# FFN up projection on Trainium2: one 512-column moving operand for both halves of x, and a sum of two bank halves on ScalarE and VectorE

## The chip, the core and the metric

The kernel runs on one core of one Trainium2 chip. The metric is the device time of one execution in microseconds. Before the change three executions gave a median of 713.83 us (712.39 to 713.88).

## What is computed

A decoder trunk of two layers over x of 256 tokens by 1024 columns, in float32. Each layer has a mixer (a short gated convolution beside an attention group) and a feed-forward part. The change touches the feed-forward part alone:

```
u = _causal_dwconv(x @ w_up[i], ffn_conv_w[i]) + ffn_conv_b[i]        # width 3, along the tokens
val, gate = u[..., :D_FF], u[..., D_FF:]                               # D_FF = 2816
x = _layer_norm(ALPHA * x + (jax.nn.silu(gate) * val) @ w_down[i], ln2_g[i], ln2_b[i])
```

## The kernel before

**Products.** A float32 product is made of three matmuls in the type f32r: each operand is split into a high part (a copy rounded to f32r) and a low part (the rest), and the product is high by high, high by low and low by high. The helper `mm3` (lines 1154, 1155 and 1156) issues the three, so these three lines carry nearly all matmuls of the kernel. The weights are split by ScalarE (`split_hi`, line 286) and VectorE (`split_lo`, line 290), unit by unit: a unit is 128 by 2048 elements. Raw units arrive by DMA from SP's queue in three buffers, and split units lie in six slots. x is split into `xh` and `xl`, each of 8 blocks (k) of 256 tokens.

**Feed-forward steps.** The 2816 inner columns are worked in 11 steps (s = 0 to 10) of 256. A step has two up units, value (v = 0) and gate (v = 1), and one down unit. For steps 1 to 10 the weights are the stationary operand and x is the moving one, so that the products come out with the inner columns on the partitions: `up` makes, for each v, two groups (c = 0 and 1, 128 inner columns each) of 8 k by 3 matmuls with 256 moving columns. Both groups of a v lie side by side in one bank, and the steps take turns: bank 4+2·odd+v. So a step may start its matmuls as soon as VectorE has finished with the step before last (`fy_done` of G-2, G counts the steps over both layers). Step 0 is done by rows (`up_rows`, x stationary), copied out by ScalarE (`copy_rows`, line 518) and transposed back (`rows_transposed`, line 1395) into banks 4 and 5.

**ScalarE and VectorE in a step.** ScalarE makes the convolution's first term with the bias from the bank (line 532, two instructions for each v), VectorE adds the other two taps from the bank (line 962, eight instructions: tap 1 of v = 0, tap 1 of v = 1, tap 2 of v = 0, tap 2 of v = 1, two groups each). Then ScalarE takes silu of the gate (line 541), VectorE multiplies (line 971), ScalarE and VectorE split the result h into `hTh` (line 548) and `hTl` (line 977); in the last step these are `qTh` and `qTl`. Between these, each of the two engines has up to three units of weights to split (`units`), at fixed places of its program: after the taps, after the product, after the split of h. GpSimd copies the step's parameters (line 693).

**Order.** Each engine's program is a fixed list. TensorE's is: rows of step 0, transposes, up 1, up 2, down 0, up 3, down 1, up 4, and so on, to up 10 and `down_last`, in which the down products of steps 8, 9 and 10 are interleaved so that the products with h of step 10 come late. VectorE's and ScalarE's program goes step by step, and each must finish step s (with its splits) before it begins step s+1:

```
up(L, 1, 1, (21, 0), (22, 0))
up(L, 2, 0, (23, 0), (24, 0))
down(L, 0, 0, (25, 0))
up(L, 3, 1, (26, 0), (27, 0))
```

Of the kernel before, what the change touches and what calls it, by code (L numbers as in the profile page):

```python
# [24 lines left out]
P = 128  # L25
D_MODEL, SEQ, DEPTH, HEAD = 1024, 256, 2, 64
KT = D_MODEL // P
# [9 lines left out]
STEPS = D_FF // (2 * P)  # L37
# [84 lines left out]
FY_CREDIT = 4  # L122

H_CREDIT = 2


def build(nc, x, w_in, short_conv_w, cmp_pe, cmp_w1, cmp_b1, cmp_w2, cmp_b2, head_norm_g, w_out, ln1_g, ln1_b,
          w_up, ffn_conv_w, ffn_conv_b, w_down, ln2_g, ln2_b, consts, out):
    fp32, f32r, bf16 = mybir.dt.float32, mybir.dt.float32r, mybir.dt.bfloat16
    ALU, ACT, AX = mybir.AluOpType, mybir.ActivationFunctionType, mybir.AxisListType  # L130

    with ExitStack() as ctx:
        def sb(name, shape, dt=fp32):
            return ctx.enter_context(nc.sbuf_tensor(name, shape, dt))

        def sem(name):
            return ctx.enter_context(nc.semaphore(name))
# [4 lines left out]
        ring_lo = [sb(f"ring_lo{i}", [P, UNIT], f32r) for i in range(SLOTS)]  # L142
        x_tok = sb("x_tok", [P, TT, D_MODEL])

        xh = sb("xh", [P, KT, SEQ], f32r)
        xl = sb("xl", [P, KT, SEQ], f32r)
        hTh = sb("hTh", [P, 2, 2, SEQ], f32r)
        hTl = sb("hTl", [P, 2, 2, SEQ], f32r)
        qTh = sb("qTh", [P, NPAIR, SEQ], f32r)
# [25 lines left out]
        part = work[:, 1024:2048].rearrange("p (t f) -> p t f", t=TT)  # L175
        ffn_y = work[:].rearrange("p (s v c n) -> p s v c n", s=2, v=2, c=2)
# [30 lines left out]
        conv_y = sb("conv_y", [P, 2, SEQ])  # L207
        conv_o = sb("conv_o", [P, 4, SEQ])

        conv_sq = sb("conv_sq", [P, 2, SEQ])  # L210
        rope_a, rope_b = (conv_sq[:, n, 0:14 * ROPE].rearrange("p (h d) -> p h d", h=14) for n in range(2))
        cstat = sb("cstat", [P, 2, TT, 4])
# [10 lines left out]
        rstd = sb("rstd", [P, TT])  # L223
        CMP_BANK = (7, 2)

        XT_BANK, MIX_BANK, X1T_BANK, ROWS_BANK, FFN_BANK = (4, 6), (4, 0), (4, 2), (6, 0), (0, 2)
        bank = [ctx.enter_context(nc.psum_tensor(f"bank{i}", [P, 512], fp32)) for i in range(8)]


# [29 lines left out]
        ln_stats, ln_root = sem("ln_stats"), sem("ln_root")  # L259
        step_par_in, fy_init = sem("step_par_in"), sem("fy_init")  # L260
        fy_mid, fy_done = sem("fy_mid"), sem("fy_done")
        rows_done, rows_copied, rows_T = sem("rows_done"), sem("rows_copied"), sem("rows_T")
        silu_done, h_done, h_hi, h_lo = sem("silu_done"), sem("h_done"), sem("h_hi"), sem("h_lo")
        y2_done = sem("y2_done")
        passed = sem("passed")
        dve_seq, pool_seq = sem("dve_seq"), sem("pool_seq")


        def xT_turn(L, t, b):

# [8 lines left out]
        def unit_used(eng, L, u, i=0):  # L279

            eng.wait_ge(slot_free[slot_of(L, u)], CREDIT + slot_round(L, u, i) + 1)
# [112 lines left out]
        def _(act):  # L394
# [125 lines left out]
            def ffn_step(L, s, odd, value, gate, h_user, units, dst=None):  # L520


                G = L * STEPS + s
                act.wait_ge(step_par_in, G + 1)
                act.wait_ge(h_lo, H_CREDIT + G - 1)
                for v, u in enumerate((value, gate)):
                    if isinstance(s, int) and s == 0:
                        act.wait_ge(rows_T, 2 * L + v + 1)
                    else:
                        unit_used(act, L, *u)  # L530
                    for c in range(2):
                        ins = nc.scalar.activation(ffn_y[:, odd, v, c, :], bank[4 + 2 * odd + v][:, SEQ * c:SEQ * (c + 1)],  # L532
                                                   ACT.Identity, scale=step_par[:, odd, v, c, 2:3],
                                                   bias=step_par[:, odd, v, c, 3:4])
                    ins.then_inc(fy_init, 1)
                for u in units[0:1]:
                    if u:
                        split_hi(act, *u)
                act.wait_ge(fy_done, FY_CREDIT + 2 * G + 2)
                y = ffn_y[:, odd].rearrange("p v c n -> p v (c n)")  # L540
                nc.scalar.activation(y[:, 1], y[:, 1], ACT.Silu).then_inc(silu_done, 1)
                for u in units[1:2]:
                    if u:
                        split_hi(act, *u)
                act.wait_ge(h_done, G + 1)
                if h_user:
                    unit_used(act, L, *h_user)
                nc.scalar.activation((hTh[:, odd] if dst is None else dst).rearrange("p c n -> p (c n)"), y[:, 0],
                                     ACT.Copy).then_inc(h_hi, 1)
                for u in units[2:3]:  # L550
                    if u:
                        split_hi(act, *u)
# [171 lines left out]
        def _(dve):  # L724
            V = nc.vector
            dve.sem_inc(fy_done, FY_CREDIT)
            dve.sem_inc(h_lo, H_CREDIT)
            V.memset(warm[:], 1.0).then_inc(warm_ready, 1)
            dve.sem_inc(x_ready, 4)

# [220 lines left out]
            def ffn_step(L, s, odd, value, gate, units, hi=None, lo=None):  # L951

                G = L * STEPS + s
                for back in (1, 2):
                    for v in range(2):
                        b = bank[4 + 2 * odd + v]
                        if back == 1:
                            dve.wait_ge(fy_init, 2 * G + v + 1)
                        else:
                            dve.wait_ge(fy_mid, 2 * G + v + 1)  # L960
                        for c in range(2):
                            ins = V.scalar_tensor_tensor(ffn_y[:, odd, v, c, back:], b[:, SEQ * c:SEQ * (c + 1) - back],  # L962
                                                         step_par[:, odd, v, c, 2 - back:3 - back],
                                                         ffn_y[:, odd, v, c, back:], ALU.mult, ALU.add)
                        ins.then_inc(fy_mid if back == 1 else fy_done, 1)
                for u in units[0:1]:
                    if u:
                        split_lo(V, *u)
                dve.wait_ge(silu_done, G + 1)
                y = ffn_y[:, odd].rearrange("p v c n -> p v (c n)")  # L970
                V.tensor_tensor(y[:, 0], y[:, 0], y[:, 1], ALU.mult).then_inc(h_done, 1)
                for u in units[1:2]:
                    if u:
                        split_lo(V, *u)
                dve.wait_ge(h_hi, G + 1)
                hi, lo = (hTh[:, odd], hTl[:, odd]) if hi is None else (hi, lo)
                V.tensor_tensor(lo.rearrange("p c n -> p (c n)"), y[:, 0], hi.rearrange("p c n -> p (c n)").bitcast(fp32),
                                ALU.subtract).then_inc(h_lo, 1)
                for u in units[2:3]:
                    if u:  # L980
                        split_lo(V, *u)
# [169 lines left out]
        def _(pe):  # L1151
            def mm3(dst, ah, al, bh, bl, start, stop, **kw):

                pe.matmul(dst, ah, bh, start=start, stop=False, **kw)  # L1154
                pe.matmul(dst, ah, bl, start=False, stop=False, **kw)  # L1155
                return pe.matmul(dst, al, bh, start=False, stop=stop, **kw)  # L1156
# [232 lines left out]
            def rows_transposed(L):  # L1389

                for t in range(TT):
                    for v in range(2):
                        pe.wait_ge(rows_copied, 4 * L + 2 * t + v + 1)
                        for c in range(2):
                            ins = pe.transpose(bank[4 + v][:, SEQ * c + P * t:SEQ * c + P * (t + 1)],
                                               probs[t][:, SEQ * v + P * c:SEQ * v + P * (c + 1)], ident)
                        if t:
                            ins.then_inc(rows_T, 1)

            def up(L, s, odd, value, gate):  # L1400

                G = L * STEPS + s
                for v, u in enumerate((value, gate)):
                    wait_unit(L, *u)
                    pe.wait_ge(fy_done, FY_CREDIT + 2 * (G - 2) + v + 1)
                    wh, wl = w_view(L, u[0], KT)
                    for part in range(2):
                        for c in range(2):
                            for k in range(4 * part, 4 * part + 4):
                                ins = mm3(bank[4 + 2 * odd + v][:, SEQ * c:SEQ * (c + 1)], wh[:, k, P * c:P * (c + 1)],  # L1410
                                          wl[:, k, P * c:P * (c + 1)], xh[:, k, :], xl[:, k, :], k == 0 and c == 0, k == KT - 1,
                                          skip_group_check=True)
                    free_unit(ins, L, u[0])

            def down_product(L, s, odd, u, t, n, c):
# [53 lines left out]
            for L in range(DEPTH):  # L1469
# [6 lines left out]
                for t, first, b in in_order:  # L1476
                    tok = slice(P * t, P * (t + 1))
                    u = first + b
# [179 lines left out]
```

## Time and profile before

| | |
|---|---|
| median of three executions | 713.83 us |
| the profiled execution's own time | 709.42 us |
| its span, first to last instruction | 707.6 us |
| mean granted TensorE clock | 0.985 |
| TensorE matmul busy | 690.6 us, 98% |
| TensorE weight load busy | 631.8 us, 89% |
| VectorE busy | 492.1 us, 70% |
| ScalarE busy | 345.1 us, 49% |
| GpSimd busy | 158.6 us, 22% |
| HBM read | 115.19 MB, 164 GB/s over the span |

Matmuls are pipelined and their ends are modelled: the duration of one overlaps the next. The time that a matmul costs is therefore read from start to start, and a full busy share only says that matmuls follow one another. ScalarE and VectorE instructions of one group overlap a little too (by some 0.1 us).

### The profile page before, as it was taken

The page shows a single profiled execution, that of the slowest core. Times are in us where ns is not written, and L with a number is a line of the kernel's source. Part 1 is how long each engine was busy: PE and PEld are TensorE (multiplying, and loading weights), DVE is VectorE, ACT ScalarE, POOL GpSimd, SP SyncE. Part 2 cuts the span into 40 slices and gives each one's busy share as a digit, 9 for nine tenths or more (in the row PEclk, how much of TensorE's full clock was granted, in tenths as well). Part 3 has the DMA queues.
Part 4 walks back from the last instruction along what each step waited for, and adds up shares of the span by engine and source line. Part 5 has one row for each costly group of instructions (what it writes and reads, how often), then busy time and mean ns, then how long its engine had stood idle before and what let it go on. Part 6 is the DMA issues. An engine that isn't in the chain of part 4 may idle for free.

```text
span 707.6 us, 11957 instructions
## 1 busy us (share of the span) xinstructions
PE 690.6 (98%) x4822; PEld 631.8 (89%) x4822; DVE 492.1 (70%) x698; ACT 345.1 (49%) x492; POOL 158.6 (22%) x54
## 2 busy tenths in 40 slices
PE   8999999999999999999999999999999999999995
PEld 5899999888999999999778999988889999999994
DVE  4675768877996666666786457686869766666646
ACT  5654535414865444444347444453258555555520
POOL 0000020230174444440000000113106444444300
PEclk9999999899999999999999999997999999999998
DMA  9972443333875555556248143432357755555301
GB/s 290 323 249 62 142 156 119 120 119 106 282 241 195 191 195 196 194 188 179 78 148 269 61 150 118 152 102 78 119 200 245 269 179 179 179 178 178 119 0 60
DMA packets 87403, 116.85 MB, mean 165 GB/s; under 512 B 5230, under 2 KB 73536, under 8 KB 87360
## 3 DMA queue, kind: packets, MB, share of 16 engines
q1 hardware_dynamic: 85920, 111.85, 47.3%
q10 hardware_dynamic: 1440, 4.39, 1.8%
q8 instruction: 30, 0.49, 0.3%
q14 instruction: 13, 0.11, 0.0%
HBM read 115.19 MB, written 1.05 MB: 164 GB/s over the span
## 4 chain that ended last, share of the span: by engine, by line
PE 92%; DVE 5%; DMA 1%; issue 1%; ACT 1%; SPq 0%; DVEq 0%; ACTq 0%
PE bank L1154 28%; PE bank L1155 27%; PE bank L1156 27%; PE bank L1239 3%; PE bank L1226 2%; DMA x_tok<-in_x 1%; PE bank L1175 1%; DVE x_tok L941 1%; DVE stats L925 1%; DVE x_tok L923 1%; PE bank L1218 1%; DVE ring_lo L290 1%; DVE x_tok L949 1%; PE bank L1328 1%; PE bank L1305 0%
## 5 line engine op out<-in xcount | busy, mean ns | idle before, releaser
L290 DVE TENSOR_TENSOR ring_lo<-raw,ring_hi 128x2048 fp32r<-128x2048 f32 x102 | 232.5, 2284 | 21.6 <-ACT ring_hi L286 21.5
L1154 PE MATMUL bank<-xh,ring_hi 128*128 128x256 f32 x832 | 237.6, 286 | 0.0
L1156 PE MATMUL bank<-xh,ring_lo 128*128 128x256 f32 x832 | 235.8, 283 | 0.0
L1155 PE MATMUL bank<-xl,ring_hi 128*128 128x256 f32 x832 | 235.7, 283 | 0.0
L286 ACT ACTIVATE ring_hi<-raw 128x2048 fp32r<-128x2048 f32 x102 | 194.4, 1909 | 11.9 <-DMA raw<-in_w_in 9.1
L693 POOL COPY step_par<-ffn_par 128x16 f32 (+1 forms) x22 | 127.5, 5800 | 170.9 <-DVE work L962 170.9
L1154 PEld LDWEIGHTS bank<-xh,ring_hi 128*128 128x128 f32 x832 | 159.8, 192 | 0.9
L1155 PEld LDWEIGHTS bank<-xl,ring_hi 128*128 128x128 f32 x832 | 159.8, 192 | 0.6
L1156 PEld LDWEIGHTS bank<-xh,ring_lo 128*128 128x128 f32 x832 | 159.7, 192 | 0.0
L962 DVE SCALAR_TENSOR_TENSOR work<-bank,step_par,work 128x255 f32<-128x255 f32 (+1 forms) x176 | 72.2, 474 | 95.2 <-ACT work L532 95.1
L532 ACT ACTIVATE work<-bank,step_par 128x256 f32<-128x256 f32 x88 | 44.2, 560 | 117.1 <-PE bank L1156 117.1
L1154 PE MATMUL bank<-ring_hi,xh 128*128 128x512 f32 (+1 forms) x224 | 81.0, 362 | 3.8 <-DVE xl L754 3.8
L1154 PE MATMUL bank<-ring_hi,hTh 128*128 128x512 f32 (+1 forms) x224 | 80.8, 361 | 0.0
L1155 PE MATMUL bank<-ring_lo,hTh 128*128 128x512 f32 (+1 forms) x224 | 80.3, 359 | 0.0
L1156 PE MATMUL bank<-ring_hi,hTl 128*128 128x512 f32 (+1 forms) x224 | 80.1, 358 | 0.0
L1155 PE MATMUL bank<-ring_lo,xh 128*128 128x512 f32 (+1 forms) x224 | 77.9, 348 | 0.0
L1156 PE MATMUL bank<-ring_hi,xl 128*128 128x512 f32 (+1 forms) x224 | 77.9, 348 | 0.0
L676 POOL TENSOR_SCALAR cstat<-cstat 128x8 f32<-128x8 f32 x4 | 8.4, 2095 | 234.6 <-DVE cstat L895 234.6
L1154 PEld LDWEIGHTS bank<-ring_hi,xh 128*128 128x128 f32 x224 | 43.0, 192 | 10.8 <-DVE xl L754 3.8
L1156 PEld LDWEIGHTS bank<-ring_hi,xl 128*128 128x128 f32 x224 | 43.0, 192 | 5.3
L1155 PEld LDWEIGHTS bank<-ring_lo,xh 128*128 128x128 f32 x224 | 43.1, 192 | 5.0 <-issue 0.5
L484 ACT ACTIVATE probs<-bank,nmax 128x128 f32<-128x128 f32 (+1 forms) x64 | 26.1, 417 | 38.5 <-DVE nmax L833 38.5
(178 smaller groups left out, 785.6 us busy)
## 6 DMA issues: line engine op xcount, KB each, us to landing
raw<-in_w_up SPq DMA_DIRECT2D x44, 1024.0 KB, 5.2
raw<-in_w_down SPq DMA_DIRECT2D x22, 1024.0 KB, 5.3
raw<-in_w_in SPq DMA_DIRECT2D x21, 1024.0 KB, 5.2
raw<-in_cmp_w SPq DMA_DIRECT2D x8, 1024.0 KB, 5.9
raw<-in_w_out SPq DMA_DIRECT2D x8, 1024.0 KB, 4.9
qkv<-in_ln_g ACTq DMA_DIRECT2D x4, 512.0 KB, 3.4
qkv<-in_ln_b ACTq DMA_DIRECT2D x4, 512.0 KB, 4.9
raw<-in_w_in SPq DMA_DIRECT2D x2, 512.0 KB, 5.6
```

What stands on the lines that cost most here:

```text
L286: nc.scalar.activation(ring_hi[slot_of(L, u)][:], raw[raw_of(L, u)][:], ACT.Copy).then_inc(hi_done, 1)
L290: eng.tensor_tensor(ring_lo[slot_of(L, u)][:], raw[raw_of(L, u)][:], ring_hi[slot_of(L, u)][:].bitcast(fp32), ALU.subtract).then_inc(split ...
L484: ins = nc.scalar.activation(probs[n % 2][:, keys * j:keys * (j + 1)], bank[n % 2][:, keys * j:keys * (j + 1)], ACT.Exp, bias=nmax[:, n % ...
L532: ins = nc.scalar.activation(ffn_y[:, odd, v, c, :], bank[4 + 2 * odd + v][:, SEQ * c:SEQ * (c + 1)], ACT.Identity, scale=step_par[:, odd, ...
L676: chain.mark(nc.gpsimd.tensor_scalar(eps_out, var, mul, eps, ALU.mult, ALU.add))
L693: nc.gpsimd.tensor_copy(step_par[:, odd].rearrange("p v c k -> p (v c k)"), ffn_par[:, bass.ds(s, 1)].rearrange("p o v c k -> p (o v c k)"))\
L962: ins = V.scalar_tensor_tensor(ffn_y[:, odd, v, c, back:], b[:, SEQ * c:SEQ * (c + 1) - back], step_par[:, odd, v, c, 2 - back:3 - back], ...
L1154: pe.matmul(dst, ah, bh, start=start, stop=False, **kw)
L1155: pe.matmul(dst, ah, bl, start=False, stop=False, **kw)
L1156: return pe.matmul(dst, al, bh, start=False, stop=stop, **kw)
L1226: ins = pe.transpose(bank[6 + n % 2][:, P * m:P * (m + 1)], probs[n % 2][:, P * m:P * (m + 1)], ident)
L1239: ins = pe.matmul(bank[2][:, HEAD * (NPAIR * g + h):HEAD * (NPAIR * g + h + 1)], probsT[n % 2][:, P * (kb * j + b):P * (kb * j + b + 1)], ...
```

## The change

`xh` and `xl` become the two halves of one tensor `xx`. For each v, c and k, `up` now issues one matmul with the high weights and 512 moving columns (256 of `xh`, 256 of `xl`), which fills a whole bank, and one with the low weights and 256 columns of `xh` into the first half of that bank. Each group (v, c) has a bank of its own, 4+2v+c, in every step. The second half of the bank is copied by ScalarE to `up_y` (a new name for `conv_o`), VectorE adds the first half to it, and the convolution then reads `up_y` in place of the bank. VectorE finishes both taps of v = 0 before v = 1. The matmuls of a group wait for VectorE's sum of the same group of the step before (`up_sum`, with a credit of four for the first step). Step 0 has no sums; its rows are transposed into banks 2 and 3.

```diff
-        xh = sb("xh", [P, KT, SEQ], f32r)
-        xl = sb("xl", [P, KT, SEQ], f32r)
+        xx = sb("xx", [P, 2, KT, SEQ], f32r)
+        xh, xl = xx[:, 0], xx[:, 1]
...
+        def up_source(s, v, c):
+
+            if isinstance(s, int) and s == 0:
+                return bank[ROWS_T_BANK[v]][:, SEQ * c:SEQ * (c + 1)]
+            return up_y[:, 2 * v + c, :]
+
+        def sums_before(L, s):
+            return 4 * (L * (STEPS - 1) + s - 1)
...
@@ ScalarE, ffn_step
-                        unit_used(act, L, *u)
+                        act.wait_ge(fy_done, FY_CREDIT + 2 * (G - 1) + v + 1)
+                        for c in range(2):
+                            if c == 0:
+                                act.wait_ge(up_half, sums_before(L, s) // 2 + v + 1)
+                            else:
+                                unit_used(act, L, *u)
+                            nc.scalar.activation(up_y[:, 2 * v + c, :], bank[4 + 2 * v + c][:, SEQ:2 * SEQ], ACT.Copy).then_inc(up_low, 1)
+                        act.wait_ge(up_sum, SUM_CREDIT + sums_before(L, s) + 2 * v + 2)
                     for c in range(2):
-                        ins = nc.scalar.activation(ffn_y[:, odd, v, c, :], bank[4 + 2 * odd + v][:, SEQ * c:SEQ * (c + 1)],
+                        ins = nc.scalar.activation(ffn_y[:, odd, v, c, :], up_source(s, v, c),
...
@@ VectorE, ffn_step
-                for back in (1, 2):
-                    for v in range(2):
-                        b = bank[4 + 2 * odd + v]
+                for v, u in enumerate((value, gate)):
+                    if not (isinstance(s, int) and s == 0):
+                        for c in range(2):
+                            dve.wait_ge(up_low, sums_before(L, s) + 2 * v + c + 1)
+                            y = up_y[:, 2 * v + c, :]
+                            V.tensor_tensor(y, y, bank[4 + 2 * v + c][:, 0:SEQ], ALU.add).then_inc(up_sum, 1)
+                    for back in (1, 2):
...
@@ TensorE
-                            ins = pe.transpose(bank[4 + v][:, SEQ * c + P * t:SEQ * c + P * (t + 1)],
+                            ins = pe.transpose(bank[ROWS_T_BANK[v]][:, SEQ * c + P * t:SEQ * c + P * (t + 1)],
...
-                    pe.wait_ge(fy_done, FY_CREDIT + 2 * (G - 2) + v + 1)
                     wh, wl = w_view(L, u[0], KT)
-                    for part in range(2):
-                        for c in range(2):
-                            for k in range(4 * part, 4 * part + 4):
-                                ins = mm3(bank[4 + 2 * odd + v][:, SEQ * c:SEQ * (c + 1)], wh[:, k, P * c:P * (c + 1)],
-                                          wl[:, k, P * c:P * (c + 1)], xh[:, k, :], xl[:, k, :], k == 0 and c == 0, k == KT - 1,
-                                          skip_group_check=True)
+                    for c in range(2):
+                        pe.wait_ge(up_sum, SUM_CREDIT + sums_before(L, s) - 4 + 2 * v + c + 1)
+                        dst = bank[4 + 2 * v + c]
+                        for k in range(KT):
+                            pe.matmul(dst[:], wh[:, k, P * c:P * (c + 1)], xx[:, :, k, :], start=k == 0, stop=False)
+                            ins = pe.matmul(dst[:, 0:SEQ], wl[:, k, P * c:P * (c + 1)], xh[:, k, :], start=False, stop=k == KT - 1)
+                        if c == 0:
+                            ins.then_inc(up_half, 1)
```

## Rows read from the trace of the kernel before

**Rows 1.** The chain that ended last, share of the span by engine

```profile
PE 92%; DVE 5%; DMA 1%; issue 1%; ACT 1%; SPq 0%; DVEq 0%; ACTq 0%
```

**Rows 2.** TensorE's timeline (start, duration, engine, line): ends of up 4, down 2

```profile
222.63 0.28 PE L1154 MATMUL bank<-xh,ring_hi 128*128 128x256 f32 x1
...
234.14 0.40 PE L1154 MATMUL bank<-ring_hi,hTh 128*128 128x512 f32 x1
...
239.61 0.28 PE L1154 MATMUL bank<-xh,ring_hi 128*128 128x256 f32 x1
```

**Rows 3.** TensorE's timeline: matmuls with 24-column weights, the first and the next

```profile
39.18 0.28 PE L1154 MATMUL bank<-xh,gate_wh 128*24 128x256 f32 x1
...
41.93 0.28 PE L1154 MATMUL bank<-xh,ring_hi 128*128 128x256 f32 x1
```

**Rows 4.** TensorE's timeline: first matmul of up 1, layer 0 and layer 1

```profile
177.06 0.36 PE L1154 MATMUL bank<-xh,ring_hi 128*128 128x256 f32 x1
...
524.06 0.36 PE L1154 MATMUL bank<-xh,ring_hi 128*128 128x256 f32 x1
```

**Rows 5.** ScalarE's timeline: begin of its step 1, layer 0 and layer 1

```profile
189.64 1.92 ACT L532 ACTIVATE work<-bank,step_par 128x256 f32<-128x256 f32 x4
...
537.74 1.91 ACT L532 ACTIVATE work<-bank,step_par 128x256 f32<-128x256 f32 x4
```

**Rows 6.** VectorE's timeline: end of step 0 and begin of step 1, both layers

```profile
183.06 3.21 DVE L962 SCALAR_TENSOR_TENSOR work<-bank,step_par,work 128x255 f32<-128x255 f32 x8
...
191.19 0.68 DVE L977 TENSOR_TENSOR hTl<-work,hTh 128x512 fp32r<-128x512 f32 x1
191.80 3.20 DVE L962 SCALAR_TENSOR_TENSOR work<-bank,step_par,work 128x255 f32<-128x255 f32 x8
...
539.89 3.21 DVE L962 SCALAR_TENSOR_TENSOR work<-bank,step_par,work 128x255 f32<-128x255 f32 x8
```

**Rows 7.** Instructions like the added ones: ns min/median/max, first and last start, forms

```profile
L1018 DVE TENSOR_TENSOR work<-bank,par x8: 397/398/399, 51.1 to 397.4; 128x240 f32<-128x240 f32 x8
...
L518 ACT ACTIVATE probs<-bank x8: 383/384/385, 165.0 to 523.4; 128x256 f32<-128x256 f32 x8
```

**Rows 8.** VectorE's timeline: two taps of the mixer's convolution, in the changed order

```profile
70.60 1.79 DVE L779 SCALAR_TENSOR_TENSOR conv_y<-conv_z,par,conv_y 128x255 f32<-128x255 f32 x4
```

**Rows 9.** Stretches: us, busy PE, PEld, DVE, ACT, POOL, then PEclk, DMA share, GB/s

```profile
130.50:137.33 6.83, 6.83 (x28) 6.37 (x29) 5.73 (x18) 2.83 (x3) 2.32 (x2) 0.52 0.91 299
475.24:485.48 10.24, 10.24 (x45) 9.55 (x44) 7.27 (x19) 2.83 (x3) 2.93 (x2) 0.51 0.63 204
...
699.60:703.90 4.30, 0.00 (x0) 0.00 (x0) 4.04 (x8) 0.00 (x0) 0.88 (x1) 0.98 0.20 74
703.95:707.60 3.65, 0.00 (x0) 0.00 (x0) 0.84 (x2) 0.00 (x0) 0.00 (x0) 0.50 0.39 146
168.50:170.30 1.80, 0.19 (x2) 0.00 (x0) 0.67 (x2) 1.58 (x4) 0.00 (x0) 1.00 0.22 82
```

**Rows 10.** VectorE's timeline: taps and last split of step 3, layer 0

```profile
218.42 2.43 DVE L962 SCALAR_TENSOR_TENSOR work<-bank,step_par,work 128x255 f32<-128x255 f32 x6 [4.88 <-ACT work L532]
...
226.37 2.28 DVE L290 TENSOR_TENSOR ring_lo<-raw,ring_hi 128x2048 fp32r<-128x2048 f32 x1
```

**Rows 11.** Last step of layer 1: VectorE's timeline, then TensorE's

```profile
684.27 2.43 DVE L962 SCALAR_TENSOR_TENSOR work<-bank,step_par,work 128x255 f32<-128x255 f32 x6 [4.80 <-ACT work L532]
...
688.80 0.69 DVE L977 TENSOR_TENSOR qTl<-work,qTh 128x512 fp32r<-128x512 f32 x1 [0.70 <-ACT qTh L548]
...
683.02 0.40 PE L1154 MATMUL bank<-ring_hi,hTh 128*128 128x512 f32 x1
...
689.85 0.39 PE L1154 MATMUL bank<-ring_hi,qTh 128*128 128x512 f32 x1
```

More of the change, by code:

```diff
@@ L124 @@
 H_CREDIT = 2
+SUM_CREDIT = 4
 def build(nc, x, w_in, short_conv_w, cmp_pe, cmp_w1, cmp_b1, cmp_w2, cmp_b2, head_norm_g, w_out, ln1_g, ln1_b,
@@ L208, in build @@
         conv_o = sb("conv_o", [P, 4, SEQ])
+        up_y = conv_o
         conv_sq = sb("conv_sq", [P, 2, SEQ])
@@ L224, in build @@
         CMP_BANK = (7, 2)
-        XT_BANK, MIX_BANK, X1T_BANK, ROWS_BANK, FFN_BANK = (4, 6), (4, 0), (4, 2), (6, 0), (0, 2)
+        XT_BANK, MIX_BANK, X1T_BANK, ROWS_BANK, ROWS_T_BANK, FFN_BANK = (4, 6), (4, 0), (4, 2), (6, 0), (2, 3), (0, 2)
         bank = [ctx.enter_context(nc.psum_tensor(f"bank{i}", [P, 512], fp32)) for i in range(8)]
@@ L261, in build @@
         fy_mid, fy_done = sem("fy_mid"), sem("fy_done")
+        up_half, up_low, up_sum = sem("up_half"), sem("up_low"), sem("up_sum")
         rows_done, rows_copied, rows_T = sem("rows_done"), sem("rows_copied"), sem("rows_T")
@@ L727, in _ @@
             dve.sem_inc(h_lo, H_CREDIT)
+            dve.sem_inc(up_sum, SUM_CREDIT)
             V.memset(warm[:], 1.0).then_inc(warm_ready, 1)
@@ L961, in ffn_step @@
                         for c in range(2):
-                            ins = V.scalar_tensor_tensor(ffn_y[:, odd, v, c, back:], b[:, SEQ * c:SEQ * (c + 1) - back],
+                            ins = V.scalar_tensor_tensor(ffn_y[:, odd, v, c, back:], up_source(s, v, c)[:, 0:SEQ - back],
                                                          step_par[:, odd, v, c, 2 - back:3 - back],
@@ L1400, in up @@
             def up(L, s, odd, value, gate):
-                G = L * STEPS + s
                 for v, u in enumerate((value, gate)):
                     wait_unit(L, *u)
-                    pe.wait_ge(fy_done, FY_CREDIT + 2 * (G - 2) + v + 1)
                     wh, wl = w_view(L, u[0], KT)
-                    for part in range(2):
-                        for c in range(2):
-                            for k in range(4 * part, 4 * part + 4):
-                                ins = mm3(bank[4 + 2 * odd + v][:, SEQ * c:SEQ * (c + 1)], wh[:, k, P * c:P * (c + 1)],
-                                          wl[:, k, P * c:P * (c + 1)], xh[:, k, :], xl[:, k, :], k == 0 and c == 0, k == KT - 1,
-                                          skip_group_check=True)
+                    for c in range(2):
[6 more added lines that the diff above has]
+                            ins.then_inc(up_half, 1)
                     free_unit(ins, L, u[0])
```

## The prediction

> **What bounds the kernel now.** I read the chain of waits first: 92% of the span is TensorE's [rows 1], so the time is the sum of TensorE's start-to-start distances, and what helps or hurts is what changes these or makes a hole between them. The busy share cannot tell a distance, since matmuls overlap; TensorE's timeline can. Up 4 has 96 matmuls of 256 columns, from 222.63 to 234.14: 11.51/96 = 119.9 ns each. Down 2, which follows, has 24 of 512 columns in 239.61 - 234.14 = 5.47 us: 227.9 ns each [rows 2]. At the full clock of 2.4 GHz, 256 columns stream in 106.7 ns and 512 in 213.3 ns, so one matmul pays about 13 to 14 ns over its streaming at either width. That is what the change goes for. Then I read the stretch around up 1 and up 2, because the change takes away the second set of banks, and there two up products follow each other with no down between. ScalarE comes to step 1 at 189.64 us [rows 5] and VectorE at 191.80 [rows 6], while up 1 began at 177.06 [rows 4]: both engines lag by a whole unit there, and before the change nothing of TensorE's waited for them.
>
> **TensorE's matmuls.** Steps 1 to 10 of two layers have 20 x 2 x 2 x 8 = 640 places (v, c, k). At each, two matmuls of 256 columns (2 x 119.9 = 239.8 ns) become one of 512 (227.9 ns): 11.9 ns less, 640 x 11.9 = 7.6 us. The low-weight matmul stays at 119.9. A step's up goes from 11.51 to 32 x 0.3478 = 11.13 us. The trace has no alternation of a 512-column and a 256-column matmul, so I bound it. From below: the 24 matmuls with 24-column weights and 256 moving columns of layer 0 take (41.93 - 39.18)/24 = 114.6 ns each [rows 3], so if the load of the low weights, which now runs beside a 512-column stream, lets its matmul come at 114.6, another 640 x 5.3 = 3.4 us goes. From above: the two segments of the moving operand are read as two passes and the 512-column matmul costs 239.8, gain nothing. I take 7.6, since the 512-column matmuls of down always have that cover for their loads and still pay 14 ns.
>
> By the Trainium skill ("TensorE: Matmul & The Clock Gate", section "Back-to-back issue gap") a 256-column matmul takes 262 cycles and a 512-column one 518 at the full clock. By it a pair would save 2.5 ns and the whole 1.6 us, as an estimate from that page; the trace does not agree with it, with 119.9 against 109.2 ns.
>
> **The hole before up 2.** The new wait: group (0,0) of up 2 needs VectorE's sum of group (0,0) of step 1. Behind that wait the whole TensorE list is queued. When can VectorE do that sum? Its program is in order: it must first end step 0 (taps, two splits, product, hTl), and step 0 adds nothing but the new order of taps, with a wait for completion between tap 1 and tap 2 of the same v. Four such taps take 1.79 us in the mixer [rows 8], against half of 3.21, about 1.64 with the overlap [rows 6]: 0.15 for each v, 0.3 for the step. So VectorE is free at 191.80 + 0.3 = 192.1; ScalarE's copy was ready long before (189.64 + 0.38) [rows 5, 7]. The sum takes 0.40 [rows 7], so TensorE goes on at 192.5. Up 1 now ends at 177.06 + 0.09 + 11.13 = 188.3. Hole: 4.2 us. In layer 1 the same: 539.89 + 0.3 + 0.4 = 540.6 [rows 6], against 524.06 + 0.09 + 11.13 = 535.3 [rows 4]: 5.3 us. Together 9.5. Nothing in the trace lets VectorE come earlier, so this has a narrow bound, 9.0 to 10.
>
> **After the hole.** The next groups of up 2 need their sums 2.8 us apart; VectorE has (0,1) at 192.9, then ScalarE's first term, four taps (1.79), and (1,0), (1,1) at about 196.4: in time for 198.1 and 200.9. Step 1 goes on: ScalarE's first term to 197.4, taps to 199.3, split to 201.5, product, split to 204.3, hTl 205.0, and the first sum of step 2 at 205.4. Up 3 asks for it at 192.5 + 11.1 + 5.5 = 209.1: 3.7 us to spare, in both layers. From then on VectorE ends its last split 11.5 us after the end of its up unit (step 3: up 3 ends some 1.3 us before the taps of 218.42, the last split at 226.37 + 2.28 = 228.65) [rows 10], and the next up but one starts 22 us after it. The four added copies (0.38 each) and sums (0.40) and the two waits make a step of VectorE about 1.6 us longer, of ScalarE 1.5: hidden under TensorE's 16.6 us per step, and if that cover were gone it would be 10 steps of 1.6. Loads on SP's queue follow the splits; those of step 1 come up to 4 us later, as TensorE does, with units 28 and later not asked for before 220 us. No DMA and nothing on GpSimd is added or moved.
>
> **The last step.** There h must be ready in time for the late products. VectorE ends at 688.80 + 0.69 = 689.49, TensorE asks at 689.85: 0.36 us to spare [rows 11]. The new chain adds a copy (0.38), a sum (0.40) and two handovers (0.04 each, estimated from the distance of ScalarE's and VectorE's rows), 0.87 in all, and has four taps (1.79) behind the last fill in place of six (2.43): + 0.23. Still covered, by 0.1; if it tips over, it costs 0.1 to 0.3 a layer. I take 0.
>
> **The clock.** The trace has the clock at half for 6.83 us and for 10.24 us, in stretches with few moving columns [rows 9]. And it has 4.3 us at the end with no matmul at all, at the end of which the clock fell to half; a hole of 1.8 us did not do it [rows 9]. The two new holes are 4.2 and 5.3 us. So I expect the clock to fall to 1.2 GHz in or just after each, and up 2 to run at half rate for a while. Price: nothing (it does not fall) to half of 10.24 = 5.1 us for each hole. With the shorter stretch, all at work, it is 3.4; but a part of it lies in the hole, where it costs nothing. I take the middle, 1.8 each, 3.6 in all. TensorE being later only widens the other engines' slack.
>
> **Sum.** - 7.6 + 9.5 + 3.6 = + 5.5 us against the profiled execution's own 709.42 (span 707.6 and 1.8 around it): 714.9. That execution lies 4.4 under the median of the runs; against 713.83 it is 719.3. 0.2% is 1.4 us, about what a measurement of this kernel can tell from no change.
>
> **Rivals.**
> (a) The holes come, the clock stays up: - 7.6 + 9.5 = + 1.9, 715.7, or 715.0 with a slightly shorter hole, on the edge of what can be told. For it: each hole is short next to those of the mixer's weak stretches, and nothing but the end of the run shows a fall after a pure hole. Against: that one, at 4.3 us. 0.12.
> (b) Faster: the low-weight matmul comes at 114.6 ns because its load is covered. Place: all 640 pairs; price: 3.4 us more, gain 11.0; it decides only if the clock also stays up: - 11.0 + 9.5 = - 1.5, 712.3, and from a pair of under 340 ns on the total is at or below zero. For it: the 256-column rows are the ones in which a load of 128 columns has as long as its stream. Against: down's own 14 ns. 0.09.
> (c) The pair saves next to nothing, because what a 256-column matmul pays beyond streaming is owed to its load and the 512-column one pays it as well: gain 1.6, then - 1.6 + 9.5 + 3.6 = + 11.5, 725.3. The mechanism would be a load that delays whichever matmul follows; the rows of down against those of up speak against it. 0.05. It is the outcome by the section named above.
> (d) The change does not do what it says: the two segments make the 512-column matmul cost 239.8. + 13.1, 726.9. 0.03.
>
> **How the numbers follow.** Forecast 0.71, (a) 0.12, (b) 0.09, (c) 0.05, (d) 0.03. The forecast's own range is 716.5 to 724 (clock 0.7 to 4 a hole). The range asked for takes in (a) and some error of the median, and leaves out (b) and most of (c) and (d): 713.8 to 724.5. Faster: (b) and a tail of (a), 0.10. Same: most of (a), 0.10. Slower: 0.80.
>
> **What the profile after would show.** TensorE: 640 matmuls fewer; 348 ns from one 512-column matmul to the next in up; a hole of about 4 us near 188 us and of about 5 us in layer 1, ended by VectorE's sum; no hole before up 3; the clock at half behind the holes. ScalarE and VectorE: 80 copies and 80 sums at 0.38 and 0.40. No wait in `down_last`. I am wrong if VectorE's first sum of step 1 comes before TensorE asks for it, if a pair costs other than 340 to 355 ns, or if the clock row stays full through both holes.

## The result and the profile after

The changed kernel takes 720.13 us in the median of four executions (716.61 to 723.11), the one before 713.11 us beside it on the same chip. The medians are 7.0 us apart, a quotient of 1.0098; the ratio on record, which is not the quotient of the medians (here and in the experiments), is 1.0118 with a 95% interval of 1.0069 to 1.0166. So the change is slower, by some 5 to 12 us. A second comparison on another chip (further down) gives 1.011. Two of the four executions took 716.6 and 717.5 us at a mean granted clock of 0.980, the other two 722.8 and 723.1 us at 0.972 and 0.971 (where these lost their clock is not known, since no trace of them was taken), so the median lies between two groups. The profiled execution has a span of 714.6 us against 707.6, and a time of its own of 717.49 against 709.42: 1.1 us of the difference between the times lie outside the span.

The page of the changed kernel, its first part and the two groups of up (columns as in the page: busy us, mean ns of one, idle time before it and what ended it):

```profile
PE 689.8 (97%) x4182; PEld 599.2 (84%) x4182; DVE 526.8 (74%) x778; ACT 374.7 (52%) x572; POOL 71.0 (10%) x54
...
L1435 PE MATMUL bank<-xx,ring_hi 128*128 128x512 f32 x640 | 229.1, 401 | 8.4 <-DVE conv_o L981 8.4
...
L1436 PE MATMUL bank<-xx,ring_lo 128*128 128x256 f32 x640 | 180.6, 282 | 0.0
```

TensorE has 640 matmuls fewer, as the change says, and the 512-column group has 8.4 us of idle time before it, all ended by VectorE's sum (line 981). The kernel before had no such idle time in its up groups. TensorE's timeline shows both places (start, duration, in brackets the idle time before it and what ended it):

```profile
187.59 0.28 PE L1436 MATMUL bank<-xx,ring_lo 128*128 128x256 f32 x1
192.07 0.77 PE L1435 MATMUL bank<-xx,ring_hi 128*128 128x512 f32 x1 [4.20 <-DVE conv_o L981]
...
538.22 0.28 PE L1436 MATMUL bank<-xx,ring_lo 128*128 128x256 f32 x1
542.69 0.47 PE L1435 MATMUL bank<-xx,ring_hi 128*128 128x512 f32 x1 [4.20 <-DVE conv_o L981]
```

The first line of each pair is the last matmul of up 1, the second the first of up 2. With 0.12 us for the matmul before, the hole is 4.36 us in both layers. VectorE's timeline of the same time answers to [rows 6]: it ends step 0 and goes straight to the two sums, with no idle time before them.

```profile
188.71 2.28 DVE L304 TENSOR_TENSOR ring_lo<-raw,ring_hi 128x2048 fp32r<-128x2048 f32 x1
190.91 0.68 DVE L1003 TENSOR_TENSOR hTl<-work,hTh 128x512 fp32r<-128x512 f32 x1
191.51 0.74 DVE L981 TENSOR_TENSOR conv_o<-conv_o,bank 128x256 f32<-128x256 f32 x2
```

Behind the holes the clock is at half. The stretches of the changed kernel (us, busy time and count of PE, PEld, DVE, ACT, POOL, then PEclk, DMA share, GB/s); the first three are the hole, the time at half clock and the rest of up 2 in layer 0, the last two the first 3.9 us of up 2 and its rest in layer 1:

```profile
187.71:192.07 4.36, 0.16 (x2) 0.03 (x1) 4.36 (x6) 1.93 (x4) 0.53 (x1) 0.95 0.75 245
192.07:195.02 2.95, 2.95 (x9) 2.56 (x10) 1.75 (x5) 1.63 (x4) 0.00 (x0) 0.50 1.03 366
195.02:204.60 9.58, 9.58 (x57) 8.43 (x56) 8.36 (x12) 6.52 (x8) 2.20 (x1) 1.00 0.27 86
...
542.69:546.60 3.91, 3.91 (x13) 3.37 (x14) 2.61 (x7) 1.70 (x5) 0.00 (x0) 0.56 0.95 331
546.60:555.44 8.84, 8.84 (x52) 7.71 (x51) 7.73 (x10) 6.46 (x8) 2.20 (x1) 1.00 0.27 82
```

In layer 0 the clock fell 3.9 us after the last matmul and stayed at half for 3.41 us; only 2.95 us of that hit working matmuls. In layer 1 it fell 0.5 us after TensorE had gone on (at 543.17), and all of its 3.41 us at half hit working matmuls. Up 2 takes 204.60 - 192.07 = 12.53 us and 555.44 - 542.69 = 12.75 us, where up 1, at full clock, takes 11.18 and 11.19 in this execution.

And the later ups. Up 3 of the changed kernel, to be held against up 4 in [rows 2] (11.51 us):

```profile
210.08 0.39 PE L1435 MATMUL bank<-xx,ring_hi 128*128 128x512 f32 x1
210.31 0.28 PE L1436 MATMUL bank<-xx,ring_lo 128*128 128x256 f32 x1
210.42 0.40 PE L1435 MATMUL bank<-xx,ring_hi 128*128 128x512 f32 x1
...
221.37 0.40 PE L1180 MATMUL bank<-ring_hi,hTh 128*128 128x512 f32 x1
...
226.87 0.39 PE L1435 MATMUL bank<-xx,ring_hi 128*128 128x512 f32 x1
```

11.29 us for 32 pairs, 352.8 ns a pair; the 16 ups from step 3 on all take 11.29. In up 1 a pair takes 347 ns, but the first 0.43 us. The down products between take 5.50 us in place of 5.47.

**Where the 7.0 us of span come from.** From the first matmul of up 1 to the first of down 0 it is 28.07 and 28.29 us in place of 23.12 in both layers: + 10.1, namely 2 x 4.36 of hole, 1.35 and 1.57 of half clock (first experiment), less 0.8 in each layer for the matmuls. Sixteen ups of 11.29 in place of 11.51: - 3.5. Downs: + 0.5. `down_last`: + 0.2 in each layer. Start and mixer: about - 0.5. Sum + 7.0.

### The profile page after: what moved, and what is told of

Read it like the earlier page. It is cut to its first block, busy times and chain, and to the rows that moved or that the text cites. A ratio compares the mean times of both kernels' runs of the same rounds, so it can differ in the third digit from the quotient of the medians.

```text
span 714.6 us, 10992 instructions
## 1 busy us (share of the span) xinstructions
PE 689.8 (97%) x4182; PEld 599.2 (84%) x4182; DVE 526.8 (74%) x778; ACT 374.7 (52%) x572; POOL 71.0 (10%) x54
## 4 chain that ended last, share of the span: by engine, by line
PE 89%; DVE 9%; ACT 1%; issue 1%; DVEq 0%; ACTq 0%
PE bank L1435 19%; PE bank L1180 17%; PE bank L1182 16%; PE bank L1181 16%; PE bank L1436 10%; PE bank L1265 3%; DVE ring_lo L304 3%; PE bank L1252 2%; PE bank L1201 1%; DVE work L988 1%; DVE x_tok L963 1%; DVE stats L947 1%; DVE x_tok L945 1%; PE bank L1244 1%; PE bank L1489 1%
## 5 line engine op out<-in xcount | busy, mean ns | idle before, releaser
L1435 PE MATMUL bank<-xx,ring_hi 128*128 128x512 f32 x640 | 229.1, 401 | 8.4 <-DVE conv_o L981 8.4
L1436 PE MATMUL bank<-xx,ring_lo 128*128 128x256 f32 x640 | 180.6, 282 | 0.0
L1435 PEld LDWEIGHTS bank<-xx,ring_hi 128*128 128x128 f32 x640 | 121.6, 190 | 38.5 <-issue 9.0
L1436 PEld LDWEIGHTS bank<-xx,ring_lo 128*128 128x128 f32 x640 | 122.3, 191 | 0.6
L988 DVE SCALAR_TENSOR_TENSOR work<-conv_o,step_par,work 128x255 f32<-128x255 f32 (+1 forms) x160 | 70.3, 481 | 47.9 <-ACT work L553 46.5
L1180 PE MATMUL bank<-ring_hi,xx 128*128 128x512 f32 (+1 forms) x224 | 80.9, 361 | 3.7 <-DVE xx L776 3.7
L1182 PE MATMUL bank<-ring_hi,xx 128*128 128x512 f32 (+1 forms) x224 | 78.0, 348 | 0.0
L1181 PE MATMUL bank<-ring_lo,xx 128*128 128x512 f32 (+1 forms) x224 | 77.9, 348 | 0.0
L714 POOL COPY step_par<-ffn_par 128x16 f32 (+1 forms) x22 | 39.8, 1817 | 256.0 <-DVE work L988 256.0
L1180 PE MATMUL bank<-xx,ring_hi 128*128 128x256 f32 x192 | 56.0, 292 | 0.0
L1181 PE MATMUL bank<-xx,ring_hi 128*128 128x256 f32 x192 | 54.3, 283 | 0.0
L1182 PE MATMUL bank<-xx,ring_lo 128*128 128x256 f32 x192 | 54.3, 283 | 0.0
L1180 PEld LDWEIGHTS bank<-ring_hi,xx 128*128 128x128 f32 x224 | 43.0, 192 | 10.8 <-DVE xx L776 3.8
L1182 PEld LDWEIGHTS bank<-ring_hi,xx 128*128 128x128 f32 x224 | 43.0, 192 | 5.4
```

What stands on the lines that cost most here:

```text
L714: nc.gpsimd.tensor_copy(step_par[:, odd].rearrange("p v c k -> p (v c k)"), ffn_par[:, bass.ds(s, 1)].rearrange("p o v c k -> p (o v c k)"))\
L988: ins = V.scalar_tensor_tensor(ffn_y[:, odd, v, c, back:], up_source(s, v, c)[:, 0:SEQ - back], step_par[:, odd, v, c, 2 - back:3 - back], ...
L1435: pe.matmul(dst[:], wh[:, k, P * c:P * (c + 1)], xx[:, :, k, :], start=k == 0, stop=False)
L1436: ins = pe.matmul(dst[:, 0:SEQ], wl[:, k, P * c:P * (c + 1)], xh[:, k, :], start=False, stop=k == KT - 1)
```

## The experiments

The first four of the eight kernels ran on one chip, the last four on another; each is compared with runs of the kernel before on its own chip. Since the mixer has stretches of half clock of changing length (first experiment), I read the variants by stretches, from the first matmul of up 1 to the first of down 0, besides the ratio.

### 1. The hole filled, so that only the clock differs

```diff
                 up(L, 1, 1, (21, 0), (22, 0))
+                keep_busy(bank[0], 19)
                 up(L, 2, 0, (23, 0), (24, 0))
```

> The changed kernel with 19 idle-time matmuls (bf16, 512 columns, 0.216 us each at full clock, 4.1 us) between up 1 and up 2, so that the wait for VectorE's sum stays but TensorE is not idle in it. Theory (hole plus clock): the wait still ends at the same time, but the clock no longer falls behind it; up 2 takes 11.1 us in place of 12.5 and 12.75, so the span goes from 714.6 to about 711.5, and the executions of 722 to 723 us do not show up again. Rival (the clock has no part of its own): span 714.6 as before, and the spread of the executions stays.

Measured: 715.41 us against 709.16, ratio 1.0073 (1.0044 to 1.0102), nine executions from 712.99 to 718.16; the profiled span is 716.4. The 19 matmuls read the tile `warm` and write bank 0; nobody reads their product. TensorE's timeline, then two stretches (the one of the 19 matmuls, and up 2) and the stretch of the mixer at half clock:

```profile
187.90 4.27 PE L1489 MATMUL bank<-warm 128*128 128x512 bf16 x19
192.05 0.47 PE L1435 MATMUL bank<-xx,ring_hi 128*128 128x512 f32 x1
...
203.23 0.39 PE L1180 MATMUL bank<-ring_hi,hTh 128*128 128x512 f32 x1
```

```profile
187.90:192.05 4.15, 4.15 (x21) 1.81 (x20) 4.15 (x6) 1.73 (x4) 0.33 (x1) 1.00 0.73 226
192.05:203.23 11.18, 11.18 (x66) 9.79 (x65) 8.77 (x14) 8.16 (x12) 2.20 (x1) 1.00 0.40 132
...
471.20:491.68 20.48, 20.32 (x84) 19.05 (x85) 13.01 (x27) 6.38 (x11) 3.70 (x2) 0.50 0.31 102
```

Up 2 starts at the same time (192.05 against 192.07) and takes 11.18 us instead of 12.53 in layer 0, and 11.17 instead of 12.75 in layer 1. That is the clock's part, 1.35 and 1.57 us. The span is not the 711.5 that I expected, for a reason outside the change: in layer 1 the mixer ran 20.48 us at half clock, where the profile of the changed kernel has 10.24 and that of before 10.24 [rows 9]. From the first matmul of the first `down_last` to up 1 of layer 1 it took 193.0 us against 188.2, so 4.8 us more; without these the span is 711.6. The nine executions end at 718.2 and none reaches 722, as expected, but they ran on a faster chip, so I count that for little.

### 2 and 3. VectorE and ScalarE relieved before the sum

One, and then both, of step 0's weight splits move to step 1 on both engines (shown for VectorE and the second variant; the splits after the third of a step go to its end):

```diff
-                ffn_step(L, 0, 0, (19, 0), (20, 0), [(L, 25), (L, 26)])
-                ffn_step(L, 1, 1, (21, 0), (22, 0), [(L, 27), (L, 28)])
-                ffn_step(L, 2, 0, (23, 0), (24, 0), [(L, 29), (L, 30), (L, 31)])
+                ffn_step(L, 0, 0, (19, 0), (20, 0), [])
+                ffn_step(L, 1, 1, (21, 0), (22, 0), [(L, 25), (L, 26), (L, 27)])
+                ffn_step(L, 2, 0, (23, 0), (24, 0), [(L, 28), (L, 29), (L, 30), (L, 31)])
```

> The changed kernel with one of step 0's two weight splits (unit 26) moved on both engines from step 0 to step 1, and step 1's second one to step 2. Theory: VectorE comes to the first sum 2.2 us sooner, so each hole shrinks from 4.35 to about 2.2 us; a hole this short leaves the clock up, as the one of 1.8 us did in the trace of before. Span 714.6 - 4.4 - 3.1 = 707.1. If the clock falls all the same: 710.2. Rival (the hole is set by something else than VectorE's place in its program, as ScalarE's copy or the credit): 714.6.

> The changed kernel with both of step 0's weight splits moved to step 1 and step 1's two to step 2. Theory: VectorE is at the first sum before up 1 ends, so there is no hole and no fall of the clock in either layer: 714.6 - 8.7 - 3.1 = 702.8, faster than the kernel before by about 5 us. Rival (the single set of banks costs time at other places too, and the delayed splits make down 0 or up 3 wait): up to 3 us more than that.

Measured with one split moved: 712.79 us against 709.16, ratio 1.0059 (1.0035 to 1.0083). TensorE's timeline at both holes, then up 2 of both layers as stretches, and the first 4.9 us of the one in layer 0 in two parts:

```profile
192.33 0.47 PE L1435 MATMUL bank<-xx,ring_hi 128*128 128x512 f32 x1 [2.58 <-DVE conv_o L981]
...
543.56 0.47 PE L1435 MATMUL bank<-xx,ring_hi 128*128 128x512 f32 x1 [2.58 <-DVE conv_o L981]
```

```profile
192.33:205.21 12.88, 12.88 (x64) 11.15 (x65) 10.47 (x17) 8.15 (x12) 2.20 (x1) 0.87 0.34 124
543.56:554.92 11.36, 11.36 (x64) 9.87 (x65) 8.94 (x14) 8.16 (x12) 2.20 (x1) 1.00 0.25 90
...
192.33:193.82 1.49, 1.49 (x9) 1.31 (x10) 0.33 (x2) 1.27 (x4) 0.00 (x0) 1.00 1.03 423
193.82:197.23 3.41, 3.41 (x13) 2.92 (x12) 2.27 (x6) 1.43 (x5) 0.00 (x0) 0.50 0.17 68
```

The hole shrank by 1.6 us, not 2.2: reckoned from the start of up 1, TensorE goes on only 1.4 us sooner (14.12 us behind it in place of 15.54), because VectorE now waits 0.70 us for ScalarE's `hTh`, and up 1 itself took 0.2 us longer. And my expectation that so short a hole leaves the clock up held in one layer only: behind the same hole the clock fell in layer 0, though only 1.5 us after TensorE had gone on (0.87 over up 2, 12.88 us), and stayed up in layer 1 (1.00, 11.36 us). So a hole of 2.7 us may or may not cost the clock, at 1.5 us a time.

Measured with both moved: 711.53 against 709.16, ratio 1.0024 (0.9997 to 1.0051), which is no gain over the kernel before where I had expected 5 us. The hole is still there, at 1.53 us. VectorE's timeline says why, and TensorE's shows the hole and a second wait, before up 4:

```profile
184.53 3.46 DVE L988 SCALAR_TENSOR_TENSOR work<-bank,step_par,work 128x255 f32<-128x255 f32 x8
188.68 0.69 DVE L997 TENSOR_TENSOR work<-work 128x512 f32<-128x512 f32 x1 [0.70 <-ACT work L562]
190.07 0.69 DVE L1003 TENSOR_TENSOR hTl<-work,hTh 128x512 fp32r<-128x512 f32 x1 [0.70 <-ACT hTh L569]
```

```profile
191.24 0.47 PE L1435 MATMUL bank<-xx,ring_hi 128*128 128x512 f32 x1 [1.37 <-DVE conv_o L981]
...
225.25 0.47 PE L1435 MATMUL bank<-xx,ring_hi 128*128 128x512 f32 x1 [0.40 <-DVE conv_o L981]
```

I had counted VectorE's work in step 0 and forgotten its chain: without the splits between, it waits 0.70 us for silu and 0.70 for `hTh`. The clock stayed up behind these shorter holes in both layers, and up 1 to down 0 takes 23.89 us in both: 4.2 and 4.4 less than in the changed kernel. The late splits cost 0.6 us before up 4: one of them waited for its raw weights. These two losses in each layer, and 2 us more before the first up (where the mixer of layer 0 had 10.24 us at half clock in place of 6.83), are why the span is 709.1 and not 702.8.

### 4. The joined matmul undone, the rest of the change kept

```diff
-                            pe.matmul(dst[:], wh[:, k, P * c:P * (c + 1)], xx[:, :, k, :], start=k == 0, stop=False)
+                            pe.matmul(dst[:, 0:SEQ], wh[:, k, P * c:P * (c + 1)], xh[:, k, :], start=k == 0, stop=False, ...)
+                            pe.matmul(dst[:, SEQ:], wh[:, k, P * c:P * (c + 1)], xl[:, k, :], start=False, stop=False, ...)
```

> The changed kernel with the one 512-column matmul of each pair undone into two of 256 columns, banks, sums and waits as in the change. Theory (the joined matmul saves 13 ns a pair in steps 1 and 2 and 7 ns in the 16 others): each up takes 11.51 us again, that is 1.7 + 3.5 = 5.2 us more, less 0.4 us in each layer because up 1 ends later and the hole shrinks: span about 719.0. Rival (the join saves nothing like that, and the sums' traffic is what costs): 714.6 to 716.

Measured: 723.62 us against 709.16, ratio 1.0189 (1.0153 to 1.0226), profiled span 717.3. TensorE's timeline, first matmul of up 3 and of down 1:

```profile
210.62 0.28 PE L1435 MATMUL bank<-xx,ring_hi 128*128 128x256 f32 x1
...
222.13 0.40 PE L1180 MATMUL bank<-ring_hi,hTh 128*128 128x512 f32 x1
```

11.51 us again for every up from step 3 on, to the hundredth what the kernel before has [rows 2], with the sums and copies running beside it. So the join is worth 0.22 us a step there, and ScalarE's and VectorE's added traffic does not slow these matmuls. Down products are back at 5.47 us too. The holes remain, 3.94 us in layer 0 and 4.75 in layer 1. The first is 0.4 us shorter, as expected; the second is longer, because in step 0 ScalarE waited for raw weights there, which put VectorE later:

```profile
529.92 1.92 ACT L300 ACTIVATE ring_hi<-raw 128x2048 fp32r<-128x2048 f32 x1 [1.09 <-DMA raw<-in_w_up]
```

The span is 2.7 us over the changed kernel's, not 4.4: the mixer before layer 1's up was 2.0 us shorter in this execution.

### 5. The changed kernel again, beside the next three

> The changed kernel itself once more, beside the three variants of this job, since the time of an execution differs from chip to chip. Theory: from the first matmul of up 1 to the first of down 0 it takes 28.1 and 28.3 us again (22.2 of matmuls, a hole of 4.35 and 1.4 to 1.7 of half clock); the hole's length is set by VectorE's program and stays, the half clock behind it may last longer in some executions. Ratio to before 1.008 to 1.014. Rival (the 28 us were chance): a stretch of another length, the hole included.

Measured: 719.39 us (716.65 to 723.03, seven executions) against 710.61; ratio 1.011 (1.0072 to 1.0148). Up 1 to down 0: 28.30 and 28.45 us, with TensorE busy for 24.1 and 24.2 of them and a mean clock of 0.94:

```profile
176.88:205.18 28.30, 24.09 (x130) 20.74 (x130) 24.22 (x32) 20.08 (x25) 4.29 (x2) 0.94 0.64 217
527.78:556.23 28.45, 24.24 (x131) 20.86 (x131) 24.38 (x32) 20.02 (x25) 4.28 (x2) 0.94 0.64 218
```

The hole is 4.37 us, as before. One thing differs: behind the half clock the pairs of up 2 take 353 ns in both layers, where the first profile of this kernel has 347. Three pairs of it, in layer 0:

```profile
195.64 0.40 PE L1435 MATMUL bank<-xx,ring_hi 128*128 128x512 f32 x1
...
196.70 0.40 PE L1435 MATMUL bank<-xx,ring_hi 128*128 128x512 f32 x1
```

So one and the same program shows both distances in up 2.

### 6. The sums of step 1 ahead of step 0's splits

The two copies and sums of step 1's value go to right behind the first term and the taps of step 0; those of step 1's gate to the head of step 1. VectorE's side (`add_halves` holds the changed kernel's wait and sum; ScalarE's copies move the same way, and step 1's no longer wait for the taps of step 0, which do not read `up_y`):

```diff
+                first, second = (isinstance(s, int) and s == n for n in (0, 1))
+                if second:
+                    add_halves(L, 1, 1)
                 for v, u in enumerate((value, gate)):
-                    if not (isinstance(s, int) and s == 0):
...
+                    if not first and not second:
+                        add_halves(L, s, v)
...
                         ins.then_inc(fy_mid if back == 1 else fy_done, 1)
+                if first:
+                    add_halves(L, 1, 0)
                 for u in units[0:1]:
```

> The changed kernel with the two copies and two sums of step 1's value moved ahead of step 0's weight splits and silu, and those of step 1's gate ahead of step 1's first term and taps; nothing else moves. Theory: VectorE has sum (0,0) 0.4 us after the taps of step 0, before up 1 ends, and (1,0) and (1,1) before up 2 asks for them, so up 1 and up 2 follow each other: 22.3 us from up 1 to down 0 in both layers in place of 28.1 and 28.3, no half clock there, span 11.8 below the changed kernel's 714.6 for the same mixer: 702.8; ratio to before 0.993 to 0.996. Rival (a single set of banks makes a hole somewhere near in any case): the time comes back as a wait before down 0 or up 3.

Measured: 705.73 us against 710.61, ratio 0.9906 (0.9868 to 0.9943); profiled span 703.6. VectorE's timeline, and up 1 to down 0 of both layers as stretches:

```profile
184.46 3.46 DVE L1003 SCALAR_TENSOR_TENSOR work<-bank,step_par,work 128x255 f32<-128x255 f32 x8
187.84 0.74 DVE L986 TENSOR_TENSOR conv_o<-conv_o,bank 128x256 f32<-128x256 f32 x2
188.50 2.29 DVE L304 TENSOR_TENSOR ring_lo<-raw,ring_hi 128x2048 fp32r<-128x2048 f32 x1
```

```profile
178.46:201.15 22.69, 22.69 (x130) 19.68 (x130) 20.96 (x29) 18.92 (x23) 2.29 (x2) 1.00 0.70 240
521.79:544.49 22.70, 22.70 (x131) 19.69 (x130) 20.97 (x29) 18.93 (x23) 2.29 (x2) 1.00 0.70 239
```

TensorE is busy through both stretches, the clock is at 1.00, and they are 5.4 and 5.6 us shorter than the 28.07 and 28.29 of the changed kernel (5.6 and 5.75 than those of experiment 5). They take 22.7 us and not the 22.3 that I expected, because both ups ran at 353 ns a pair. No wait came back at another place: the downs and later ups have the changed kernel's distances. With the same single set of banks, the same copies and sums, and every split in its old step, the hole is gone. So the banks alone do not make it; the order of VectorE's and ScalarE's programs does.

### 7 and 8. The matmuls of a group by width, alone and with the sums early

```diff
                         for k in range(KT):
                             pe.matmul(dst[:], wh[:, k, P * c:P * (c + 1)], xx[:, :, k, :], start=k == 0, stop=False)
+                        for k in range(KT):
                             ins = pe.matmul(dst[:, 0:SEQ], wl[:, k, P * c:P * (c + 1)], xh[:, k, :], start=False, stop=k == KT - 1)
```

> The changed kernel with the eight 512-column matmuls of a group first and then its eight 256-column ones, in place of pairs. Rival P (the 353 ns per pair of steps 3 to 10 belongs to the alternation of widths): each width keeps its own distance, 226.6 and 119.9 ns, a group takes 2.77 us, an up 11.09 us in all steps, 0.2 us less in each of 16 steps, span about 3.2 us less than 714.6. Rival Q (it comes from the banks that ScalarE and VectorE read beside TensorE, or from the memory): up 3 and later stay at 11.3 us.

> Both of the two edits before. Theory with P: no hole and 11.09 us per up, 22.3 us for the first two and 0.2 us less in 16 steps: span about 699.6, ratio to before 0.989 to 0.992. With Q: as the variant without grouping, 702.8 and 0.993 to 0.996.

Measured, grouping alone: 716.66 us, ratio 1.0072 (1.0042 to 1.0102). TensorE's timeline, up 3 from its first matmul to the first of down 1, with the change of width in its first group:

```profile
210.67 0.84 PE L1435 MATMUL bank<-xx,ring_hi 128*128 128x512 f32 x3
...
212.48 1.11 PE L1437 MATMUL bank<-xx,ring_lo 128*128 128x256 f32 x8
213.44 0.63 PE L1435 MATMUL bank<-xx,ring_hi 128*128 128x512 f32 x2
...
221.82 0.40 PE L1180 MATMUL bank<-ring_hi,hTh 128*128 128x512 f32 x1
```

Eight 512-column matmuls in 1.81 us (226 ns), eight 256-column ones in 0.96 (120 ns), an up in 11.15 us against 11.29. Rival P is borne out: the 353 ns come with the alternation, though an alternation at 347 ns a pair costs no more than the grouped matmuls (346). The gain is 0.14 us an up, not 0.2, since a grouped up took 11.15 us and not the 11.09 expected. Its profiled span of 717.3 is no contradiction: the mixer had 20.48 us at half clock in layer 1 again. Both edits together: 703.30 us against 710.61, ratio 0.9873 (0.9831 to 0.9915), six executions from 700.00 to 707.10, span 702.0, up 1 to down 0 in 22.42 and 22.41 us:

```profile
176.53:198.95 22.42, 22.42 (x131) 19.76 (x130) 20.69 (x28) 18.86 (x22) 2.29 (x2) 1.00 0.71 242
521.82:544.23 22.41, 22.41 (x130) 19.74 (x130) 20.68 (x28) 18.85 (x22) 2.29 (x2) 1.00 0.71 242
```

The span is 702.0 and not the 699.6 expected, mostly from the smaller gain of the grouping and a mixer before layer 1's up that was 1.7 us longer than in the changed kernel. This version beats the kernel before by about 1.3% and the changed one by some 2.3% (0.9873 / 1.011). Whether the grouping adds to the early sums is not shown by the medians, whose intervals overlap; the stretches show it, 0.3 us for the first two ups and 0.14 us for each later one.

## Why the prediction was right

The forecast was + 5.5 us and 719.3; measured + 7.0 of span (+ 8.1 of the profiled executions' own times) and 720.13 in the median, within the range and on the side that was forecast. The two places, the wait and the clock were right; the matmuls' gain was too large, and that the total came so near is partly luck, as the end of this section says. By its terms:

- **The hole before up 2** (predicted 4.2 and 5.3 us, together 9.5): 4.36 in both layers, 8.7. The sum began at 191.51 and TensorE went on at 192.07, where the prediction had 192.1 and 192.5 (the whole execution was 0.5 us early by then). Layer 1 was mis-sized by 0.9: in the trace of before, VectorE's lag there held a wait of ScalarE for raw weights (shown below), which came again in neither profile of the changed kernel, so both layers had the same lag. It did come again in experiment 4, and there layer 1's hole was 4.75 us. Experiments 2, 3 and 6 tie the hole to VectorE's place in its program: it shrank as work was taken from before the sum and went with the sum's move.

```profile
527.01 1.91 ACT L286 ACTIVATE ring_hi<-raw 128x2048 fp32r<-128x2048 f32 x1 [1.39 <-DMA raw<-in_w_up]
```

- **The clock** (predicted 1.8 each, 3.6): 1.35 and 1.57, 2.9 together: by so much up 2 got shorter when the hole was filled (experiment 1). Rival (a), in which the clock stays up, did not come.
- **The matmuls** (predicted - 7.6): this is the term that was mis-sized. The pair did cost less than three 256-column matmuls, but 352.8 ns in the sixteen ups from step 3 on, and 347 in the other four of this execution, against the 347.8 of the prediction. Up 1 and up 2 gave 0.8 us in each layer and the sixteen ups 3.5, the downs lost 0.5: - 4.5. The step that failed is the sum of the two distances, "A step's up goes from 11.51 to 32 x 0.3478 = 11.13 us", taken for all twenty steps: it holds when the widths are grouped (11.15) and where the alternation runs at 347 ns, not in the sixteen others, nor in every execution in the first two steps (experiments 5 and 6). Rival (b), a cheaper low-weight matmul, came in part: at 347 ns a pair the two are 230 and 117 ns apart, but of what the second saves on its 119.9 the first loses most on its 227.9. Rivals (c) and (d) would need pairs of 357 and 360 ns (2.5 ns and nothing under three times 119.9), in the mean, which no profile shows; by experiment 4 the join is worth 0.22 us a step in 16 steps and 0.4 in up 1.
- **After the hole**: no hole before up 3, as worked out; the first sum of step 2 came at 204.46 and up 3 asked at 210.08.
- **The last step** (0.1 us to spare, or 0.1 to 0.3 lost): it tipped. `qTl` ends at 345.70 and the products with h of step 10 begin at 345.85, 0.15 us behind it, as TensorE went on 0.16 us behind the end of the sum (191.91) before up 2. By the third of them TensorE is 0.15 us later than in the same place before; with 0.04 lost earlier the whole of `down_last` is 0.2 us longer, in each layer.

```profile
345.01 0.69 DVE L1003 TENSOR_TENSOR qTl<-work,qTh 128x512 fp32r<-128x512 f32 x1 [0.70 <-ACT qTh L569]
```

```profile
345.56 0.39 PE L1182 MATMUL bank<-ring_hi,hTl 128*128 128x512 f32 x1
345.85 0.47 PE L1180 MATMUL bank<-ring_hi,qTh 128*128 128x512 f32 x1
```

The errors partly cancelled: 0.8 less hole, 0.7 less clock and 0.5 at the start and in the mixer against 3.1 less gain from the matmuls and 0.4 in `down_last`, together the 1.5 us between + 5.5 and + 7.0. And the 0.8 us between 719.3 and 720.13 say little, since the median of four lies between two groups 6 us apart. The prediction took 1.4 us for what a measurement can tell; the interval of this one is 3.5 us to either side.

## What to carry to other kernels

When a change takes away the second set of buffers, look for a place where the producer comes twice in a row, and read there how far the consumer lags in its fixed program: here the lag cost nothing before and became a hole. The holes of about 4 us in TensorE cost more than themselves, 1.4 to 1.6 us of half clock each. Here they were closed by moving the small releasing instructions (a copy and a sum, 0.4 us each) ahead of long ones that nobody waited for; moving the long ones instead left 1.5 us of hole and made a new wait later.

## What the runs showed of the hardware that was not expected

- **Two widths in alternation run in one of two patterns.** At full clock a pair of 512 and 256 columns took 347 ns in up 1 and up 2 of the changed kernel's first profile and 352.8 ns in every later up; grouped, 226 and 120 ns. The first two ups are not tied to the fast one: up 2 was slow in both layers of the second profile of the same program (experiment 5), and both ups were slow in experiment 6 (22.69 us for 64 pairs, 353 ns). Up 4 of experiment 3, behind its wait, was fast in both layers (11.17 us). The downs between the later ups take 5.50 us in place of 5.47. What puts TensorE into the one or the other was not tried.
- **The same hole, with and without a fall of the clock.** 2.7 us: once it fell, 1.5 us after TensorE had gone on, once not, in one execution (experiment 2). 3.9 to 4.8 us: it fell behind all eight in the profiles (the changed kernel twice, experiments 4 and 7). 1.5 us: behind none of two (experiment 3).
- **The clock in the mixer differs from execution to execution** on its own: in layer 1 the profiles show 10.24 us at half clock in the kernel before and in both profiles of the changed one, 20.48 in experiments 1 and 7 and 3.41 in experiments 4 and 6, though the experiments changed nothing in the mixer. From the first matmul of the first `down_last` to up 1 of layer 1 it took between 186.3 us (experiments 4 and 6) and 193.1 (experiment 7), 188.0 in the kernel before. That is why spans of single profiles had to be read by stretches.
- **GpSimd's copy of the step's parameters** (128 x 16) takes 1.8 us in the mean in place of 5.8, 7.60 us for one before and 2.10 after at the same place of the steady steps. It is off the path, and its cause was not looked for.
